# Moving the tiles of a transformer kernel to other byte offsets in a partition

## The reference, cut to what matters

```python
x = first_block(x, ...)            # h @ w_in, sigmoid(h @ w_merge[i]) * (y @ w_br[i]), merged @ w_out
for i in range(2):
    x = x + (conformer_conv(...) if i == 0 else diff_attention(...))
    x = x + memory_cross_attention(rms_norm_2(x, norm_mem[i]), mem, w_q, w_k, w_v, w_o)
    x = x + (silu(h @ w_gate) * (h @ w_up)) @ w_down
return rms_norm_2(x, norm_final)
```

## Time and profile before

| | us |
|---|---|
| median of 3 timed runs | 1140.58 |
| lowest and highest of them | 1140.39, 1140.6 |
| profiled execution: its span, first to last instruction | 1136.0 |
| TensorE busy (matmul) in it | 1106.3 |
| weight loads busy in it | 951.5 |
| VectorE busy in it | 759.4 |
| ScalarE busy in it | 549.2 |

### The profile page before, as it was taken

One profiled execution on the slowest core, in us unless ns is written; L12 is line 12 of the kernel. 1 busy time (PEld: TensorE's weight loads), 2 busy tenths in 40 slices (PEclk: granted clock), 3 DMA queues, 4 the chain that ended last, 5 costly groups with the idle time before them and its releaser, 6 DMA issues.

```text
span 1136.0 us, 15034 instructions
## 1 busy us (share of the span) xinstructions
PE 1106.3 (97%) x6141; PEld 951.5 (84%) x6141; DVE 759.4 (67%) x1049; ACT 549.2 (48%) x782; POOL 49.2 (4%) x82
## 2 busy tenths in 40 slices
PE   3999999999999999999999999999999999999997
PEld 3689978787898887988988988788988989888886
DVE  4637676865679997545688845556967545778642
ACT  2347654344350446655444544556765545444442
POOL 3021000000010000001000000000011000000000
PEclk9999999999999999999999999999999999999999
DMA  9965354755665405534655555544445335555450
GB/s 322 352 192 167 129 189 146 269 177 168 220 172 156 141 4 183 185 112 146 178 176 175 192 196 190 178 170 149 148 149 183 127 116 186 186 185 186 162 171 38
DMA packets 118358, 195.08 MB, mean 172 GB/s; under 512 B 6297, under 2 KB 39217, under 8 KB 118288
## 3 DMA queue, kind: packets, MB, share of 16 engines
q1 hardware_dynamic: 115728, 187.51, 49.7%
q0 software_dynamic: 2560, 6.60, 2.1%
HBM read 193.04 MB, written 1.05 MB: 171 GB/s over the span
## 4 chain that ended last, share of the span: by engine, by line
PE 91%; DVE 4%; ACT 2%; DMA 1%; issue 1%; POOL 1%; SPq 0%; ACTq 0%; DVEq 0%; POOLq 0%
PE product L629 56%; PE product L666 5%; PE small L666 5%; PE product L2443 5%; PE product L668 3%; PE small L668 3%; PE small L2467 2%; PE product L931 2%; ACT w_high L553 1%; PE small L776 1%; PE small L2008 1%; DMA w_raw<-in_w_ada 1%; PE small L691 1%; PE small L1378 1%; PE small L2029 1%
## 5 line engine op out<-in xcount | busy, mean ns | idle before, releaser
L563 DVE TENSOR_TENSOR w_low<-w_raw,w_high 128x2048 fp32r<-128x2048 f32 (+3 forms) x160 | 349.9, 2190 | 181.8 <-ACT w_high L553 180.2
L553 ACT ACTIVATE w_high<-w_raw 128x2048 fp32r<-128x2048 f32 (+3 forms) x160 | 292.9, 1832 | 187.2 <-PE product L629 151.0
L629 PE MATMUL product<-w_high,H 128*128 128x512 f32 (+2 forms) x736 | 239.5, 393 | 0.0
L629 PEld LDWEIGHTS product<-w_high,H 128*128 128x128 f32 x736 | 137.9, 188 | 28.5 <-issue 2.2
L629 PE MATMUL product<-H,w_high 128*128 128x256 f32 x816 | 154.0, 286 | 0.2 <-ACT queries_keys L1025 0.2
L629 PE MATMUL product<-w_low,H 128*128 128x512 f32 (+2 forms) x368 | 142.4, 387 | 0.0
L629 PEld LDWEIGHTS product<-H,w_high 128*128 128x128 f32 x816 | 128.9, 191 | 2.2 <-issue 1.3
L629 PE MATMUL product<-H,w_low 128*128 128x256 f32 x408 | 115.7, 284 | 0.0
L666 PE MATMUL product<-H,w_high 128*128 128x512 f32 x256 | 90.8, 399 | 0.0
L666 PE MATMUL small<-H,w_high 128*128 128x512 f32 x256 | 90.8, 399 | 0.0
L629 PEld LDWEIGHTS product<-w_low,H 128*128 128x128 f32 x368 | 69.3, 188 | 11.8 <-issue 0.2
(11 more groups left out here) (394 smaller groups left out, 1736.4 us busy)
## 6 DMA issues: line engine op xcount, KB each, us to landing
w_raw<-in_ffn_w_gate SPq DMA_DIRECT2D x20, 1024.0 KB, 5.1
w_raw<-in_ffn_w_up SPq DMA_DIRECT2D x20, 1024.0 KB, 5.1
w_raw<-in_ffn_w_down SPq DMA_DIRECT2D x20, 1024.0 KB, 5.0
w_raw<-in_w_merge SPq DMA_DIRECT2D x16, 1024.0 KB, 5.1
w_raw<-in_w_ada SPq DMA_DIRECT2D x16, 512.0 KB, 9.8
w_raw<-in_mem_w_k SPq DMA_DIRECT2D x8, 1024.0 KB, 5.0
w_raw<-in_mem_w_v SPq DMA_DIRECT2D x8, 1024.0 KB, 5.1
w_raw<-in_conv_w_pw SPq DMA_DIRECT2D x16, 512.0 KB, 5.2
```

The source lines that it names most:

```text
L553: k.act.eng.activation(chunk_view(k, k.w_high[j], i), raw_of(k, i), ACT.Copy).then_inc(*k.act.tells("weights_high", ("weights high", i)))
L563: k.vec.eng.tensor_tensor(low, raw, high.bitcast(F32), ALU.subtract).then_inc(*k.vec.tells("weights_low", ("weights low", i)))
L629: mm = pe.eng.matmul(bank[:, off:off + wide], a, r, start=b not in started, stop=True, skip_group_check=True)
```

## The change

It changes addresses alone. No instruction is added, taken away or reordered. A new helper `to_line(past)` moves the allocation point to the next address that is `past` bytes past a multiple of 512. `vector_cols` (356 bytes, given 384) now comes first, so H begins at 16512 + 384 = 16896, which is 33 x 512. `common` comes behind H, so that the weight rings begin at 16896 + 16384 + 2112 = 35392, 64 past a multiple of 512. `X`, `HN`, the gains and `stats` come behind the weights (`X` begins 64 past where it began 192 past). The second block's tiles start at byte 145312 as before; `hidden` is moved to 147776 (320 past), `o_mem` to 184416 (96 past), with what lies behind them. `mem` (320 past) and `y_op` (256 past) stay.

| tile | past a multiple of 512, before | after |
|---|---|---|
| H | 32 | 0 |
| w_raw, w_high, w_low | 32 | 64 |
| hidden | 416 | 320 |
| o_mem | 416 | 96 |
| mem | 320 | 320 |
| y_op | 256 | 256 |

```diff
+LINE = 512
...
+    def to_line(self, past=0):
+
+        self.at += (past - self.at) % LINE
+
...
     def layout(self):
         w = self.w
         self.limit = self.top - 4 * FIRST_W
-        self.common = self.sb("common", [P, COMMON_W])
-        self.ident, self.ones, self.causal, self.invfreq, self.half = (
-            self.common[:, at:at + n] for at, n in (COMMON[name] for name in ("ident", "ones", "causal", "invfreq", "half")))
-        self.X, self.HN = self.sb("X", [P, NT, D]), self.sb("HN", [P, NT, D])
-        self.gains_at = self.at
-        self.gains = [self.sb(f"gain{i}", [P, D]) for i in range(2)]
-        self.stats, self.stat_at, self.st = self.sb("stats", [P, 728]), 0, {}
+        self.vector_cols = self.sb("vector_cols", [P, N_VECTOR_ROWS])
+        self.to_line()
         self.whole_conv = self.sb("whole_conv", [P, KT, S], at=self.at + 4 * KT * S)
         parts = self.sb("H", [P, 2, KT, S], F32R)
...
+        self.common = self.sb("common", [P, COMMON_W])
+        self.ident, self.ones, self.causal, self.invfreq, self.half = (
+            self.common[:, at:at + n] for at, n in (COMMON[name] for name in ("ident", "ones", "causal", "invfreq", "half")))
         self.w_raw = [self.sb(f"w_raw{i}", [P, CK * CN]) for i in range(self.N_RAW)]
...
-        self.vector_rows, self.vector_cols = self.sb("vector_rows", [N_VECTOR_ROWS, P]), self.sb("vector_cols", [P, N_VECTOR_ROWS])
+        self.X, self.HN = self.sb("X", [P, NT, D]), self.sb("HN", [P, NT, D])
+        self.gains_at = self.at
+        self.gains = [self.sb(f"gain{i}", [P, D]) for i in range(2)]
+        self.stats, self.stat_at, self.st = self.sb("stats", [P, 728]), 0, {}
+        self.vector_rows = self.sb("vector_rows", [N_VECTOR_ROWS, P])
...
         self.q_mem = self.sb("q_mem", [P, KT, S])
+        self.to_line(LINE * 3 // 16)
         o = self.pair("o_mem", KT)
...
         self.at = after_junk
+        self.to_line(LINE * 5 // 8)
         hidden = self.pair("hidden", FT)
```

## The result

| | before | after |
|---|---|---|
| median of the timed runs, us | 1140.49 (4 runs, 1140.28 to 1140.6) | 1132.16 (4 runs, 1130.84 to 1132.58) |
| profiled execution, first to last instruction, us | 1136.0 | 1129.5 |
| TensorE busy in it, us | 1106.3 | 1099.9 |

The changed kernel takes 0.9931 of the time before (95% interval 0.9917 to 0.9945): 8.3 us less. It is faster, by 0.7% and clear of the noise, but the gain is a little over a third of the 22.6 us forecast. 1132.16 lies outside the forecast's own range of 1108 to 1128, and inside the wide one of 1096 to 1141.

A forecast was written before the change was run, and what follows sets the result against it. TensorE, busy 97% of the span, was taken as the bound, through how fast matmul passes follow each other. Six terms summed to 22.6 us: 1140.6 to 1118.0 us, chance 0.55, own range 1108 to 1128, wide range 1096 to 1141.

The forecast's parts named there:

- The no-change rival: All fp32r passes: surplus is a fixed cost, addresses are worth nothing, time stays 1140.6 us; chance 0.10.
- Term 2: 512 pairs of a wide and a narrow pass (L666, L668): 353.3 to 340.0 ns, 6.8 us less.
- Term 3: 1104 passes of 512 weight columns past H: a quarter of the surplus gone, to 224.5 ns, 3.9 us less.
- The slower rival: Passes with H: distance 0 was the good one, 448 gives 234 ns; +4.2 us, 1144.8 us; chance 0.15.
- Term 1: 1224 passes of 256 H columns past weights: 119.9 to 115.0 ns, 6.0 us less.
- Term 4: 528 passes with hidden, distance from 384 to 256: to 226.7 ns, 2.8 us less.
- Term 5, o_mem: 192 passes with o_mem, distance from 384 to 32: 233.0 to 226.7 ns, 1.2 us less.
- Term 6: Stationary mem (192 passes) and y_op (96): 233.3 to 226.7 ns, 1.9 us less; moving mem (384): nothing.
- Covers: VectorE and ScalarE work beside TensorE, thinnest in gate and up: splits unchanged, 2289 ns for one, time left with faster passes.

The follow-up runs named there:

- run 1: Changed kernel with H, weight rings, hidden and o_mem all 32 bytes further, distances among them kept; 1132.71 us, ratio 0.9948 to the kernel before.
- run 2: Changed kernel with H and weights at 0, hidden and o_mem at 384 past 512, old distances except mem's and y_op's; 1137.03 us, ratio 0.9993.
- run 5: Changed kernel with H at 128, weights 64, o_mem 320, hidden 128 past 512; 1140.1 us, one run, 10.2 us of it at half clock.
- run 6: Changed kernel with H at 0, weights, o_mem and hidden all at 128 past 512; 1134.67 us against 1137.99 for the kernel before, one run each.
- run 8: Changed kernel with a 64-byte gap between H's halves, H from 128, weights at 192, hidden and o_mem at distance 0, mem moved; 1130.15 us, one run.
- run 7: Changed kernel with only o_mem moved, from distance 32 to 0 modulo 256 (320 past 512); 1130.97 us in one run.
- run 10: Changed kernel with all of H at 128, w_high at 192, w_low at 128 past 512; 1137.72 us, ratio 1.0001 to the kernel before.
- run 9: Changed kernel with H's high part at 128, low part 192, w_high 192, w_low 256; 1137.07 us, ratio 0.9993 to the kernel before.

## Why the prediction was right in its sign and wrong in its size

- **What bounds the kernel.** Right. Spans and TensorE's busy time fell by the same 6.5 and 6.4 us, no engine became busier, and the addresses of operands are what set the difference (runs 1 and 2). Against it stands the rule cited in the prediction, that TensorE's ports never wait on anyone (the Trainium skill, SBUF — State Buffer, SBUF: two separate sides): the same instructions on the same data moved by 0.5% with their addresses alone (run 1, 0.9948). Whether a port waits or something behind it, the runs don't tell. The no-change rival fell: 0.9931, with an interval that ends at 0.9945.
- **Term 2, the pairs, failed, and most.** The prediction took 340.0 ns for 353.3 and so 6.8 us, the largest term. It was 0. The 340.0 was put together from whole cycles of surplus, "16 cycles of surplus in the narrow pass and 32 in the wide one", read from rows rounded to 10 ns (0.11 and 0.23 us in the earlier trace rows). In the trace of before the pairs go round 350, 350 and 361 ns, and not one takes less than 349. In the traces the wide start to the narrow start is 236.1 ns before and 235.0 after, the narrow to the next wide 117.2 and 118.3: one gives what the other takes. At distance 64 a wide pass is at its worst level alone, too (233.3 in run 5), and no row of before had a wide pass there. What moved the pairs was 128, 351.1, more so 192, 348.9, and above all the gap in H, 346.7 (runs 6, 5 and 8).
- **Term 3, the wide passes with H, had the wrong sign.** "A quarter of the surplus gone, a guess": they rose from 227.8 to 229.3, a loss of 1.5 us where 3.9 were to be won. Its count of 1104 held 96 passes of fewer columns. The text had seen that the present distance was the best of the rows and did not follow it. The slower rival had its mechanism right, distance 0 is the good one for 512 columns, but priced 448 at 234; at 229.3 it stays under the 231.4 from which it decides.
- **Term 1** was right in kind: 116.1 for 115.0, 4.5 of 6.0 us. Part of the passes run at 113.3 ns, among them the row of 96, and part at 117.8, with the same distances.
- **Term 4** was right: 226.9 for 226.7, 2.9 for 2.8 us.
- **Term 5, o_mem**, failed: 233.2 for 226.7. The distance is 32, and what helps is 0 modulo 256, which run 7 gave (228.7).
- **Term 6** gave 1.3 of 1.9 us for the stationary side, and lost 1.0 where the moving mem was put at nothing: at distance 0 the narrow passes are at their worst level, 119.6.
- **The common flaw.** A step down was taken for every family at a new distance. Read modulo 256, not 512, the rows of before held the law in outline: hidden and mem go to distance 0, where wide passes had 228 and narrow ones 119.9. That would have given terms 4, 6 and the loss with mem. For distances 64 and 192 nothing in the trace spoke, and the value nearest the rows was no gain.
- **The time outside.** The 4.6 us between span and median were said to lie outside the passes. After the change the profiled execution's own time, 1130.84, is 1.3 us over its span, and in the runs of the experiments a time lies 1.2 to 1.4 us over its span every time. The rest was most likely the clock, and it moved; that is not shown.
- **Covers.** As said: VectorE's split still takes 2289 ns a piece, beside 2289 before, TensorE doesn't wait for it (0.2 us on its groups of the page), and the float32 passes stayed.

```profile
L572 DVE TENSOR_TENSOR w_low<-w_raw,w_high 128x2048 fp32r<-128x2048 f32 x142 | 324.6, 2289 | 166.6 <-ACT w_high L562 165.0 <-issue 1.6
```

## What to carry to other kernels

Where TensorE bounds a kernel and a matmul streams beside the next one's weight load, compare its start-to-start interval with that of the same form elsewhere in the kernel before trusting it, and list the byte distance from moving to stationary operand modulo 256 next to it: in this kernel's fp32r passes 0 was the best for 512 columns and 64 for 256. Keep one distance throughout a run of passes, as no rule priced the mixes. Price such a move by rows at the same distance, and at no gain where none exists. Then list which other tiles the move shifts against each other: here mem and y_op changed distance in kernels that meant to leave them. And when two kernels differ by under 0.5%, look at the granted clock of each timed run before the difference is given to the code.

## What was not expected of the hardware

- The interval of an fp32r pass has a period of 256 bytes in the distance of its operands: distances 256 and 0, 288 and 32, 320 and 64, 448 and 192 behave alike (runs 1, 2, 5 and 6). Between the best and the worst distance there are 6.5 ns of 227 for 512 columns and 4.7 of 115 for 256. The absolute address played no part where it was moved alone (runs 1 and 2). Why 256, the runs do not tell.
- With the same distances a stretch of narrow passes mostly settles at 113.3 or at 117.8 ns and stays there, and the same stretch can take one level in one kernel and the other in the next (changed kernel and run 7). What picks the one or the other was not found; were all of them at 113.3, the 1224 passes would give 1224 x 2.8 = 3.4 us more.
- A run of wide passes whose moving side lies at distances 0 and 192 in turn takes 232 to 233 ns, although the two alone give 227 to 228 and 229.3 (H in run 10, hidden in run 9). Distances 0 and 64 mixed in the same way give just their mean, 229.1 (hidden in run 10).
- TensorE's clock falls to its half level for 3.4 to 10.2 us, near 199 us into the kernel, in some executions and not in others of one and the same program, at a cost of some 3 us for the longer kind. What sets it off is open.
